# Score products of attention and fox: the two 64-row sets of a head issued next to each other, one mask product per bank

## The reference

```python
# differential attention: 8 heads; a head has two sets c of 64 dimensions for queries and keys
for j in range(lp // Q_BLOCK):                       # query blocks of 128 rows
    s = jnp.einsum('bhcqd,bhckd->bhcqk', qb, kb).astype(jnp.float32) * scale
    mask = (ki <= qi) & (ki >= FRONT_PAD)
    p = jax.nn.softmax(jnp.where(mask, s, NEG_INF), axis=-1)
    a = p[:, :, 0] - lam * p[:, :, 1]
    outs.append(jnp.einsum('bhqk,bhkv->bhqv', a.astype(dt), vb))

# fox: 16 heads of 64, query blocks of 128
logits = (jnp.einsum('bhqd,bhkd->bhqk', q[:, :, q0:q1], k[:, :, :q1]) * scale
          + cumf[:, :, q0:q1, None] - cumf[:, :, None, :q1])
probs = jax.nn.softmax(jnp.where(mask, logits, -jnp.inf), axis=-1)
outs.append(jnp.einsum('bhqk,bhkd->bhqd', probs, v[:, :, :q1]))
```

## Time and profile before

| | |
|---|---|
| median of 3 runs | 1429.78 us (1429.70 to 1431.85) |
| profiled execution, its time and its span | 1430.1 us, 1428.3 us |
| busy: TensorE matmul, VectorE, ScalarE | 95%, 64%, 57% of the span |
| mean granted TensorE clock | 0.978 |
| attention's score products (first and last) | 767.0 to 886.3 us |
| fox's score products (first and last) | 1305.8 to 1398.7 us |

### The profile page before, as it was taken

How to read it: one execution, slowest core, us unless ns; L and a number is a source line. 1 busy time by engine, 2 the same in 40 slices (tenths; PEclk the granted TensorE clock), 3 DMA queues, 4 the chain that set the end, 5 groups by cost and what they waited for, 6 DMA issues and landing times.

```text
span 1428.3 us, 27604 instructions
## 1 busy us (share of the span) xinstructions
PE 1358.8 (95%) x10246; PEld 1304.3 (91%) x10246; DVE 921.2 (64%) x1522; ACT 808.0 (57%) x1567; POOL 83.4 (6%) x81
## 2 busy tenths in 40 slices
PE   6999999998999999999999999799999899989997
PEld 6999999998999998999998777799989899977887
DVE  5777537857777437777446665477764575666774
ACT  6666535446666537667444444676664443556662
POOL 2000001012000002000002000220001000010000
PEclk9999999999999999999999999899999899999999
DMA  5766553653667643667533331356675254344340
GB/s 193 246 231 244 208 196 104 196 175 116 224 232 247 218 139 126 240 229 250 186 104 120 102 104 45 118 172 236 229 265 173 75 164 130 116 143 150 124 120 30
DMA packets 63314, 239.98 MB, mean 168 GB/s; under 512 B 7025, under 2 KB 8449, under 8 KB 63105
## 3 DMA queue, kind: packets, MB, share of 16 engines
q1 hardware_dynamic: 63168, 238.84, 50.5%
q0 software_dynamic: 64, 0.02, 0.0%
HBM read 237.76 MB, written 1.05 MB: 167 GB/s over the span
## 4 chain that ended last, share of the span: by engine, by line
PE 74%; DVE 12%; ACT 9%; issue 4%; DMA 2%; DVEq 0%; ACTq 0%; SPq 0%
PE bank L1735 19%; PE bank L1737 19%; PE bank L1736 19%; DVE w_lo L1045 5%; ACT w_hi L580 3%; PE bank L1742 2%; ACT ada_raw L656 2%; PE bank L1807 2%; PE bank L1808 1%; PE bank L1800 1%; PE bank L1743 1%; PE bank L2101 1%; DMA raw<-w 1%; ACT arena L989 1%; PE bank L1972 1%
## 5 line engine op out<-in xcount | busy, mean ns | idle before, releaser
L1045 DVE TENSOR_TENSOR w_lo<-raw,w_hi 128x1024 fp32r<-128x1024 f32 (+1 forms) x376 | 493.4, 1316 | 344.5 <-ACT w_hi L580 344.3
L1735 PE MATMUL bank<-x_hl,w_hi 128*128 128x272 f32 (+1 forms) x1776 | 517.1, 291 | 16.9 <-DVE w_lo L1045 16.7
L1737 PE MATMUL bank<-x_hl,w_lo 128*128 128x272 f32 (+1 forms) x1776 | 511.4, 288 | 0.0
L1736 PE MATMUL bank<-x_hl,w_hi 128*128 128x272 f32 (+1 forms) x1776 | 509.7, 287 | 0.0
L580 ACT ACTIVATE w_hi<-raw 128x1024 fp32r<-128x1024 f32 (+1 forms) x376 | 413.8, 1106 | 130.4 <-PE bank L1737 108.4
L1735 PEld LDWEIGHTS bank<-x_hl,w_hi 128*128 128x128 f32 x1776 | 336.5, 189 | 19.5 <-DVE w_lo L1045 9.8
L1736 PEld LDWEIGHTS bank<-x_hl,w_hi 128*128 128x128 f32 x1776 | 339.0, 191 | 0.6
L1737 PEld LDWEIGHTS bank<-x_hl,w_lo 128*128 128x128 f32 x1776 | 335.8, 189 | 0.0
L1735 PE MATMUL bank<-a_hi,w_hi 128*128 128x272 f32 (+1 forms) x960 | 280.5, 292 | 14.6 <-DVE a_lo L1157 3.5
L1737 PE MATMUL bank<-a_hi,w_lo 128*128 128x272 f32 (+1 forms) x960 | 276.7, 288 | 0.0
L1736 PE MATMUL bank<-a_lo,w_hi 128*128 128x272 f32 (+1 forms) x960 | 276.4, 288 | 0.0
(11 more groups left out here) (277 smaller groups left out, 1457.1 us busy)
## 6 DMA issues: line engine op xcount, KB each, us to landing
raw<-w SPq DMA_DIRECT2D x312, 512.0 KB, 4.5
raw<-w SPq DMA_DIRECT2D x64, 704.0 KB, 4.5
ada_raw<-ada_w SPq DMA_DIRECT2D x48, 512.0 KB, 3.6
h<-x_in SPq DMA_DIRECT2D x1, 1088.0 KB, 5.3
work<-bands SPq DMA_DIRECT2D x1, 544.0 KB, 6.8
cst<-consts SPq DMA_DIRECT2D x1, 528.0 KB, 4.5
out<-h SPq DMA_DIRECT2D x1, 512.0 KB, 3.0
out<-h SPq DMA_DIRECT2D x4, 128.0 KB, 2.0
```

The source lines that it names most:

```text
L1045: ve.tensor_tensor(w_lo[:, s, 0:n], raw[:, s, 0:n], w_hi[:, s, 0:n].bitcast(F32), ALU.subtract).then_inc(w_lo_ready, 1)
L1735: te.matmul(dst, w_hi[:, s, a:a + P], rhs_hi, start=first, stop=False)
L1736: te.matmul(dst, w_hi[:, s, a:a + P], rhs_lo, start=False, stop=False)
L1737: return te.matmul(dst, w_lo[:, s, a:a + P], rhs_hi, start=False, stop=last)
```

## The change

In attention the score products of the two sets are issued in turn: block A of set 0, block A of set 1, block B of set 0, block B of set 1. Then comes one mask product for each bank, which adds the mask to the diagonal 128 columns of both blocks at once. So that these lie at one distance, block B moves to columns 0 to 271 of its bank and block A to columns 272 to 415: their diagonal parts then start at column 144 and at column 288. The second product into a bank no longer has `start=True`. The maxima and the exponentials read the blocks at their new columns, in the same order and sizes. In fox the columns stay, and each bank has its two score products and then one mask product for both blocks; the two heads of a pair are not interleaved.

```diff
+        SCORE_AT = ((T, 0, KA), (0, KA, T))
...
-                    for b, (at, n) in enumerate(((0, KA), (KA, T))):
+                    for b, (src, at, n) in enumerate(SCORE_AT):
                         i = 2 * c + b
-                        sc.activation(probs[:, c, at:at + n], bank[(4, 6)[c]][:, at:at + n], ACT.Exp, scale=0.125,
+                        sc.activation(probs[:, c, at:at + n], bank[(4, 6)[c]][:, src:src + n], ACT.Exp, scale=0.125,
...
-                        ve.reduce_max(small[:, i:i + 1], bank[(4, 6)[c]][:, at:at + n], AX.X
+                        ve.reduce_max(small[:, i:i + 1], bank[(4, 6)[c]][:, src:src + n], AX.X
...
-                for c in range(2):
-                    rows = slice(64 * c, 64 * c + 64)
-                    dst = bank[(4, 6)[c]]
-                    te.matmul(dst[:, 0:KA], q_rot[b][rows, 0:P], k_rot[b][rows, 0:KA], start=True, stop=False)
-                    te.matmul(dst[:, META:KA], ident_b[:, :], causal_b[:, :], start=False, stop=True)
-                    te.matmul(dst[:, KA:KA + T], q_rot[b][rows, P:SEQ], k_rot[b][rows, 0:T], start=True, stop=False)
-                    te.matmul(dst[:, 2 * KA:KA + T], ident_b[:, :], causal_b[:, :], start=False, stop=True
+                half = [(bank[(4, 6)[c]], slice(64 * c, 64 * c + 64)) for c in range(2)]
+                for dst, rows in half:
+                    te.matmul(dst[:, T:T + KA], q_rot[b][rows, 0:P], k_rot[b][rows, 0:KA], start=True, stop=False)
+                for dst, rows in half:
+                    te.matmul(dst[:, 0:T], q_rot[b][rows, P:SEQ], k_rot[b][rows, 0:T], start=False, stop=False)
+                for c, (dst, _) in enumerate(half):
+                    both = dst[:, KA:KA + 2 * KA].rearrange("p (a t) -> p a t", a=2)[:, :, 0:P]
+                    te.matmul(both, ident_b[:, :], causal_b[:, :].unsqueeze(1).broadcast_to([P, 2, P]), start=False, stop=True
                               ).then_inc(pe.step(f"s{h}", f"s{c}"), 1)
...
                     te.matmul(dst[:, 0:P], q_half[:, e, 0:P], k_all[:, j, e, 0:P], start=True, stop=False)
-                    te.matmul(dst[:, 0:P], ident_c, causal_c, start=False, stop=True)
-                    te.matmul(dst[:, P:3 * P], q_half[:, e, P:SEQ], k_all[:, j, e, :], start=True, stop=False)
-                    te.matmul(dst[:, 2 * P:3 * P], ident_c, causal_c, start=False, stop=True).then_inc(pe.step(f"fs{j}", f"s{e}"), 1)
+                    te.matmul(dst[:, P:3 * P], q_half[:, e, P:SEQ], k_all[:, j, e, :], start=False, stop=False)
+                    both = dst[:, :].rearrange("p (a t) -> p a t", a=2)[:, :, 0:P]
+                    te.matmul(both, ident_c, causal_c.unsqueeze(1).broadcast_to([P, 2, P]), start=False, stop=True
+                              ).then_inc(pe.step(f"fs{j}", f"s{e}"), 1)
```

More of the change, by code:

```diff
@@ L1344, in maxima @@
                     ve.wait_ge(pe.sem, pe.at(f"s{h}", f"s{c}"))
-                    for b, (at, n) in enumerate(((0, KA), (KA, T))):
+                    for b, (src, _, n) in enumerate(SCORE_AT):
                         i = 2 * c + b
-                        ve.reduce_max(small[:, i:i + 1], bank[(4, 6)[c]][:, at:at + n], AX.X
+                        ve.reduce_max(small[:, i:i + 1], bank[(4, 6)[c]][:, src:src + n], AX.X
                                       ).then_inc(vec.step(f"max{h}", "AB"[b].join(["m", str(c)])), 1)
```

## The result

The changed kernel takes 1413.11 us (median of 6 runs, 1410.04 to 1415.58) against 1429.46 us for the kernel before (6 runs, 1427.58 to 1431.85): ratio 0.9878, 95% interval 0.9866 to 0.9891. That is 16.35 us less. The forecast was 1417, 12.9 us less, with a range from 1414.5 to 1424, so the time lies outside the range, on the fast side. The profiled execution of the changed kernel took 1414.27 us, its span 1412.5 us.

A forecast was written before the change was run, and what follows sets the result against it. TensorE, with 74% of the chain and attention's scores on it, was taken as the bound; 11.2 (heads 1 to 7) + 1.5 (head 0) + 0.2 (fox) = 12.9 us off 1430.1 gave 1417 us, range 1414.5 to 1424.

The forecast's parts named there:

- The scores stand on the chain in attention: Attention's scores: time taken from TensorE there comes out of the 16.7 us period, 1.6 us per head.
- The two sets run side by side, independently: Attention's scores: row halves load weights and stream at the same time, so a head's block takes 1.14 us, not 2.73.
- The cost of a change of shape: TensorE in attention's scores: about 0.1 us unhidden weights and 0.1 emptying; eight changes take 1.05 of 2.73 us.
- Room beside it: VectorE and ScalarE beside attention's scores: the maxima just fit before the exponentials, with about 0.1 us to spare.
- Heads 1 to 7, 11.2 us: Attention's heads after the first: seven times 1.6 us saved, 11.2 us.
- Head 0, 1.5 us: Attention's first head: block ends 2.7 us earlier, but the clock is still low until 774.6, so 1.5 us saved.
- rival 5: Behind attention's head 0: denser products raise the clock before 774.6, up to 1.6 us more saved, 1415.5 us; chance 0.10.
- Fox, 0.2 us: Fox's scores: fewer mask products save 0.2 us in the last pair only and nothing in seven pairs.
- The cover: Fox's pairs: TensorE's wait for VectorE's probabilities, 7 times, 3.1 us, hides any saving in the scores.
- rival 1: Attention's scores: sets overlap but records start in program order, about 0.22 us lost per head, 1419 us; chance 0.17.

The follow-up runs named there:

- Set by set: Changed kernel, but in attention blocks A and B of set 0, then A and B of set 1, then both masks: 1412.26 us (ratio 0.9858).
- sets in turn: Changed kernel, but in attention set 0 has its two scores and merged mask before set 1 has the same: 1420.61 us (ratio 0.9934).
- the meta rows: Changed kernel, but in `head_sum` the product over the 16 meta rows moves from first to last of three: 1412.01 us (ratio 0.9860).
- fox only: Kernel before in attention, with fox as in the changed kernel: 1429.44 us (ratio 0.9996).
- head 0 old: Changed kernel, but attention head 0's scores in the old order of eight products: 1415.66 us (ratio 0.9906).

## Why the prediction was wrong in size

- **The scores stand on the chain in attention.** Right: block 1.6 us shorter, period 1.6 us shorter.
- **The two sets run side by side, independently.** Right, 1.14 us as summed. Set by set shows the overtaking, sets in turn what it is worth.
- **The cost of a change of shape, some 0.1 us for weights and 0.1 for emptying.** Right in size: the prediction's 1.05 us for eight changes is 0.13 each; measured were 0.15 each (2.74 to 2.14 us with four of them gone) and 0.2 us for the one of the meta rows.
- **Room beside it.** Right: 0.28 us between maxima and exponentials where 0.1 was expected.
- **Heads 1 to 7, 11.2 us.** Measured 11.2.
- **Head 0, 1.5 us.** This step failed. It took the low clock from 767.9 to 774.6 as given and asked only when it would rise; rival 5, too, let it fall first. But whether it falls hung on the very score block that the change shortens. Measured: 3.7 us, of which 3.0 is the fall that no longer comes and 0.7 the block. The 0.7 is less than the block's own 1.6, since head 0's VectorE and ScalarE work takes over. The fall is in all four traces with an old or half-shortened block (before, sets in turn, fox only, head 0 old) and in none of the seven with the short block. With 3.7 in place of 1.5 the forecast is 1414.8 us, just inside the range.
- **Fox, 0.2 us.** The cover holds, and the last pair gives the 0.2 us forecast. The 0.05 us for each of five pairs ahead of it was put at nothing; the totals can't be told from no change.
- **The rest.** 16.35 - 11.2 - 3.7 - 0.4 leaves 1.1 us in the medians, and these carry the time below the range. The granted clock on record for each run has room for them: it puts the kernel before at 62 us at the lower level on average (the 42 runs beside the experiments) and the changed one at 50 (6 runs). Of these 12 us fewer, 6.8 are head 0's; the other 5 would be worth some 2 us at 0.44 each, an estimate. Whether they are luck or come from the change is open.
- **The range** was too narrow below. It allowed 1.5 us either way for the clock, from three runs that differ by 2.1; here one fall was 3.0, and the 42 runs of the kernel before beside the experiments lie between 1426.96 and 1434.89 us.
- **The price of rival 1.** The prediction puts it at some 1.5 us less than the forecast; by its own sums it is 12.9 - 11.2 = 1.7. Nothing hangs on it, as set by set excludes the rival.

## What to carry to other kernels

Two float32 products that use different halves of the array's rows and different banks cost the time of one in both orders tried (alternating, or set by set), as long as no product of another shape is between them; so gather products by shape. When a change shortens thin work right behind a wait, read the granted clock there and ask whether it will fall at all, not only when it rises. Once the clock or the block is mended, look for what is next late, since a filled wait gave 3.0 us in one place and no gain that the totals show in another.

## What the runs showed of the hardware

- Records of two row halves start in the same 0.04 us, and 64-row products pass others that stand ahead of them in the program (set by set: 1.15 us for the block in either order).
- Three float32 products of no use in a wait of 1.4 us made the kernel of before 4.7 us faster (1429.43 to 1424.73), with the clock at 1.00 behind head 0 instead of 0.50 for 6.8 us; 3.0 of the 4.7 us lie at head 0.
- Two bfloat16 masks of 128 columns cost what one of 256 does, 2 x 0.06 against 0.11 us, when no other shape is between them.
